# Prompt attention on one core: the factor transposes ahead of the scores, and the second of two scored items one piece later

## The reference

```python
def nsa_core(q, qpos, ck, cv, gather_slc, n_slc, wk, wv, wpos):
    s = jnp.einsum('btghd,bngd->btghn', q, ck)
    p = masked_softmax(s, cvalid[None, :, None, None, :])
    o_cmp = jnp.einsum('btghn,bngd->btghd', p.astype(cv.dtype), cv)
    ...
    s = jnp.einsum('btghd,btgkrd->btghkr', q, sk).reshape(B, T, NSA_GROUPS, NSA_HPG, -1)
    p = masked_softmax(s, svalid)
    o_slc = jnp.einsum('btghm,btgmd->btghd', p.astype(sv.dtype), sv.reshape(B, T, NSA_GROUPS, -1, HEAD_DIM))
    s = jnp.einsum('btghd,bsgd->btghs', q, wk)
    p = masked_softmax(s, wvalid[None, :, None, None, :])
    o_win = jnp.einsum('btghs,bsgd->btghd', p.astype(wv.dtype), wv)
    return o_cmp, o_slc, o_win
...
    o_nsa = gates[:, :, 0] * o_cmp + gates[:, :, 1] * o_slc + gates[:, :, 2] * o_win
```

## Time and profile before

| | |
|---|---|
| median of 3 runs | 2266.75 us (2266.01 to 2271.41) |
| the profiled execution | 2266.64 us |
| its span | 2265.0 us |
| mean granted TensorE clock | 0.971 of full speed |
| PE busy | 2130.3 us, 94% of the span |
| DVE, POOL, ACT busy | 931.0, 544.3, 447.6 us |

### The profile page before, as it was taken

How to read it: one execution, slowest core, us unless ns; L and a number is a source line. 1 busy time by engine, 2 the same in 40 slices (tenths; PEclk the granted TensorE clock), 3 DMA queues, 4 the chain that set the end, 5 groups by cost and what they waited for, 6 DMA issues and landing times. The chain is left out here.

```text
span 2265.0 us, 32090 instructions
## 1 busy us (share of the span) xinstructions
PE 2130.3 (94%) x12018; PEld 1748.4 (77%) x12018; DVE 931.0 (41%) x1810; ACT 447.6 (20%) x983; POOL 544.3 (24%) x525
## 2 busy tenths in 40 slices
PE   5999999899788888999999999899999999999996
PEld 5978887676465556888888778688888888888885
DVE  4352114662455656321212457533333333534544
ACT  1530001422355544100000133201101010000002
POOL 5031220023411113412111564222222322000121
PEclk9999999987899999999999999999999999999998
DMA  9621213566300000112120442111111111122422
GB/s 258 179 93 38 56 38 90 156 158 178 105 1 1 1 1 20 38 29 56 28 56 19 119 119 83 38 38 55 37 37 48 45 37 37 52 91 88 154 89 91
DMA packets 244765, 161.60 MB, mean 71 GB/s; under 512 B 34659, under 2 KB 234885, under 8 KB 244590
## 3 DMA queue, kind: packets, MB, share of 16 engines
q1 hardware_dynamic: 229500, 138.85, 22.1%
q0 software_dynamic: 5008, 18.45, 2.4%
q10 hardware_dynamic: 10146, 2.80, 0.7%
HBM read 147.52 MB, written 16.71 MB: 73 GB/s over the span
## 5 line engine op out<-in xcount | busy, mean ns | idle before, releaser
L3336 DVE TENSOR_TENSOR big<-big,ps 128x264 f32<-128x264 f32 x308 | 131.8, 429 | 352.8 <-PE ps L2996 351.3
L2996 PE MATMUL ps<-hT,ring 128*128 128x264 f32 x1056 | 251.4, 388 | 10.6 <-ACT hT L3138 10.6
L3623 PE MATMUL ps<-big,ring 128*128 128x264 f32 x1056 | 240.6, 388 | 2.5 <-PEq L3851 2.5
L2996 PEld LDWEIGHTS ps<-hT,ring 128*128 128x128 f32 x1056 | 201.8, 191 | 45.8 <-ACT hT L3138 11.1
L3623 PEld LDWEIGHTS ps<-big,ring 128*128 128x128 f32 x1056 | 201.7, 191 | 37.6 <-issue 2.8
L2996 PE MATMUL ps<-big,ring 128*128 128x264 f32 x928 | 223.1, 389 | 4.3 <-PEq L3851 4.3
L210 PE MATMUL ps<-hT,ring 128*128 128x264 f32 x912 | 213.8, 392 | 3.9 <-PEq L3851 2.5
L210 PEld LDWEIGHTS ps<-hT,ring 128*128 128x128 f32 x912 | 175.8, 193 | 36.5 <-issue 4.1
L2996 PEld LDWEIGHTS ps<-big,ring 128*128 128x128 f32 x928 | 176.3, 191 | 34.5 <-issue 4.7
L210 PE MATMUL ps<-big,ring 128*128 128x264 f32 x816 | 184.7, 386 | 0.0
L210 PEld LDWEIGHTS ps<-big,ring 128*128 128x128 f32 x816 | 155.0, 190 | 26.5
(11 more groups left out here) (473 smaller groups left out, 2941.5 us busy)
## 6 DMA issues: line engine op xcount, KB each, us to landing
ring<-in_w_ada SPq DMA_DIRECT2D x44, 512.0 KB, 5.7
ring<-in_w_in SPq DMA_DIRECT2D x34, 512.0 KB, 5.0
ring<-in_w_ff_down SPq DMA_DIRECT2D x16, 1024.0 KB, 4.9
ring<-in_w_ff_gate SPq DMA_DIRECT2D x22, 512.0 KB, 4.0
ring<-in_w_ff_up SPq DMA_DIRECT2D x22, 512.0 KB, 5.2
ring<-in_w_out SPq DMA_DIRECT2D x16, 512.0 KB, 5.3
ring<-in_w_ff_down SPq DMA_DIRECT2D x8, 768.0 KB, 4.2
x_kept<-big SPq DMA_DIRECT2D x2, 2112.0 KB, 7.4
```

The source lines that it names most:

```text
L2996: ins = pe.matmul(ps[:, b, 0:NH], w[:, k, :], cols[:, k, :], start=k == 0, stop=k == 3)
L3336: dve.tensor_tensor(to, x, ps[:, bank[j], 0:NH], ALU.add).then_inc(f_joined, 1)
L3623: ins = pe.matmul(ps[:, bank(n, j), 0:NH], w[:, k, :], cols[:, k, :], start=c == 0 and k == 0, stop=c == 2 and k == h - 1)
```

## The change

In each round PE transposes the factors of the group that ended before it scores, no longer after. Of the items to be scored in a round, the first is scored there; the others follow once the round's first piece has been turned and the value product of the piece before it is done. Nothing else is changed: the operations and their number, the planner, the waits on each operation, and the lists of DVE, ACT, POOL and SP (DVE's and ACT's line numbers rise by 3).

```diff
             for x, y in enumerate(turned):
-                for z in ahead[x + 1]:
-                    score(z)
                 if x and closes(turned[x - 1]):
                     factors(group(turned[x - 1]))
+                for z in ahead[x + 1][:1]:
+                    score(z)
                 for p in of_item[y]:
                     turn(p)
                     if last is not None:
                         value(last)
+                    if p == of_item[y][0]:
+                        for z in ahead[x + 1][1:]:
+                            score(z)
                     last = p
             value(last)
```

## The result

Over 20 runs each, the changed kernel takes 2251.89 us in the median against 2268.24 us before; the ratio is 0.9934, with an interval of 0.9921 to 0.9948. Of the 2266.64 us from which the sum was made that is 15.0 us less (11.8 to 17.9), and the medians themselves lie 16.4 us apart; forecast were 16.4 us less and a time of 2250.2 us.

What follows compares the result with a forecast made beforehand. PE was taken to bound the attention, busy 249.16 of 281 us. Terms 10.7 + 2.8 + 0 + 1.3 + 1.6 = 16.4 us off 2266.64 give 2250.2 us (chance 0.80), own range 2246 to 2255, with Rival 1 to 2258.

Steps and rivals of the forecast that it cites:

- Rounds 4 and 12: Eight rounds: factor transposes fit into PE's wait for exponentials and their copy runs beside the score; 8 x 1.34 = 10.7 us.
- the tie stays a tie: At the next score PE and ACT tie; ACT's exponentials also come 1.34 us earlier, so the gain is kept.
- Rival 2: Gain given back at the next score, rounds 4 and 12 win nothing: 2262.5 us; chance 0.06.
- Round 8: Four rounds: factors push the score back 0.66 us, their copy runs beside it, turn about 0.7 us earlier; 2.8 us.
- The slack: Round 8: POOL's product and the free bank 4 are ready 0.3 us or more before the factors' transposes start.
- Rival 1: Waiting factors block the scores behind them, round 8's gain is gone: 2254.6 us, or 2257.4 if later still; chance 0.09.
- Round 7: Four rounds: splitting the scores removes no wait and costs nothing; 0 us.
- "PE's sum of work is equal": Round 7: the split leaves PE the same total work, the ground for a term of 0.
- Round 15: Three rounds: the 1.11 us wait for DVE's copy becomes about 0.7 us at the next factors; 3 x 0.44 = 1.3 us.
- The clock: Behind the compressed score's 1.11 us wait, passes 0 and 2 fall to 1.2 GHz; one of two 1.57 us falls avoided, 1.6 us.
- Rival 3: The score-to-score chain sets the pace in twelve rounds with factors, each 0.66 us longer: +7.9 us, 2274.5 us; chance 0.02.

Runs made afterwards that it cites:

- the products made later: Changed kernel, with POOL making the first of each group's two gate products twice more ahead of both, about 1.4 us later; attention 276.16 us.
- the wait put back: Changed kernel, but PE waits behind the compressed score until DVE has copied it; run twice, attention 276.62 and 278.03 us, time's ratio to before 0.9948.
- Bank 5 first: Changed kernel with round 7 unsplit and, in round 16, the compressed item's bank 5 turned ahead of bank 4; attention 269.54 us, ratio to before 0.9922.

## Why the prediction was right

The forecast was right in direction and place, and the time lies within its own range. By its terms:

- **Rounds 4 and 12**, forecast 8 x 1.34 = 10.7 us: measured 1.35 us in round 4 and 1.34 in round 12, 10.8 us. The step that mattered, that ACT's exponentials shift with the turn and the tie stays a tie, is shown by the next score, 1.35 us earlier. Rival 2 did not happen.
- **Round 8**, forecast 4 x 0.7 = 2.8 us: measured 0.76, 3.0 us. The slack was 0.52 us where the prediction had 0.3. Rival 1 did not happen; the products made later show what it would have cost.
- **Round 7**, forecast 0: this term was mis-sized. The split costs 0.19 us a pass, 0.8 us, because two small scores back to back take less time than apart. "PE's sum of work is equal" was the step that failed.
- **Round 15**, forecast 3 x 0.44 = 1.3 us with a new wait of about 0.7: measured 3 x 0.3 = 0.9 us and a wait of 0.86. DVE's copy starts where it did, 5.94 us behind the start of the compressed score, but the factors start 0.56 us behind the copy's start, where the forecast had 0.43. That the wait hangs on DVE's queue is shown by ACT's taking over the copy.
- **The clock**, forecast one fall of two avoided, 1.6 us: measured both, 3.1 us. The forecast named the right idle time, and the wait put back bears it out; but one fall of two was a choice between bounds, made because 0.7 and 0.69 us of waiting were left and because the same order had kept its clock in pass 1. Behind the waits that are left no clock fell: 0.86 us in 18 rounds, with 0.69 us behind it in 15 of them. And the clock did not fall "during the 1.11 us of waiting", as the forecast reads its rows, but at the end of it: 0.06 us behind it in pass 0, 0.02 us ahead of it in pass 2.

The measured terms make 10.8 + 3.0 - 0.8 + 0.9 + 3.1 = 17.0 us, against 17.05 in the trace of the attention. The gain of the time, 15.0 us, holds that number in its interval. That the forecast of 16.4 us comes so near is in part luck: it was 1.2 us too high in rounds 7 and 15, 0.3 too low in rounds 4, 8 and 12, and 1.5 too low for the clock. Rival 3 is out: only round 8's own score came later, by the 0.6 us that were forecast, and the next score came earlier by 0.75 us there and by 1.35 us behind round 4.

By the Trainium skill, "TensorE: Matmul & The Clock Gate", section "Step-by-step: what each phase is for", matmuls stay in program order. The trace agrees: with the products made later, PE waited 0.86 us at the factors, and the score behind them, which does not need them, came 0.92 us later.

## What to carry to other kernels

Where an engine waits twice in a row for the same other engine, put the work that causes the second wait into the first: the transposes fit into 0.99 us of waiting, and their copy ran beside the score. Before moving an instruction ahead of others in an in-order queue, count how long ago its last input was ready, for that slack (0.52 us here) is all that protects what is now behind it. And look at the clock behind idle time, too: the 1.11 us wait behind the 64-column matmuls cost up to 1.57 us more in each pass in which the clock fell.

## What the runs showed of the hardware

PE's clock fell to the 1.2 GHz level (granted clock 0.50), with 1.1 to 1.4 us of idle time behind the 2 us of 64-column matmuls and at most one small score, in 9 of 12 rounds, and not once in 21 when 128-column transposes and a value product followed at once. A fall cost 1.4 to 1.6 us.

The spread of the whole kernel's times lies ahead of the attention: in the eleven profiles it begins between 592.87 and 610.55 us, and from its end to the end of the span all take 1371.9 to 1372.8 us. In the samples' stage the granted clock differs from execution to execution. Bank 5 first and the change again, windows of 500 to 590 us:

```profile
500.00:590.00 90.00, 77.39 (x685) 0.91 0.63 178
...
500.00:590.00 90.00, 82.36 (x565) 0.75 0.59 170
```

The first reaches the attention at 597.56 us, the second at 606.67. What sets the clock there was not tried.
